# Gate and up projections of the feed-forward layers by one level of Strassen's scheme

## The chip, the cores and the metric

One Trainium2 chip, one of its cores. The metric is the device time of one launch in microseconds; the median of three runs of the kernel before is 3846.43 (3845.4 to 3850.24).

## What is computed

Three hybrid layers over 512 tokens of width 1024 in float32. Each has a large input projection, several sequence branches (state space, RWKV and HGRN in the first; mLSTM, grouped attention, windowed attention and differential attention in the other two), a gated merge with an output projection, and a feed-forward layer. The last of these is what matters here:

```python
h2 = rms_norm(x, norm2_g)
ffn = (jax.nn.silu(h2 @ w_ffn_gate) * (h2 @ w_ffn_up)) @ w_ffn_down
return x + ffn
```

with a hidden width of 2816, that is 22 tiles of 128. The first layer has the same form under other names.

## The kernel before

Activations lie with their channels on the 128 partitions and the 512 tokens along the free axis: `k.x` is 8 tiles of 128x512. A product in float32 accuracy is made of three passes (`three_passes`, L561): the upper part of the weights times the upper part of the activations, upper times lower, lower times upper (L563, L564, L565), where "upper" is the value rounded to the matmul's type (fp32r) and "lower" what is left. Weights come from HBM in chunks of 128x1024 (eight tiles of 128x128) into `k.raw`, four chunks deep (`Stream.load`, L468, issued by SyncE). ScalarE copies a chunk to its upper part (`make_hi`, L486), VectorE subtracts to get the lower part (`make_lo`, L492), each two chunks deep. A chunk is used once.

The gate/up stage is `scaled_products` (L4351): a step is one gate tile and one up tile of the hidden width, two steps to a body, 22 steps in a loop. TensorE makes 24 matmuls of 512 columns for the gate and 24 for the up tile. The norm's weight is multiplied into the activations ahead (`SplitAhead`, L1598, beside the output projection of the merge); the norm's factor per token, `rstd`, is applied afterwards: VectorE multiplies the gate out of PSUM by it (L4430), ScalarE applies Silu (L4409), GpSimd multiplies by `rstd` once more for the up side (L4452), VectorE multiplies by the up tile out of PSUM (L4442), ScalarE and VectorE split the hidden tile (L4413, L4435). `ScaledEnd` (L4303) does this for the last hidden tile inside the down projection.

The output projection `w_out` runs in `project` (L885), with `SquareSum` (L1457: squares on ScalarE, L1480; their sums on GpSimd, L1491) and `SplitAhead` (L1624 on ScalarE, L1633 on VectorE) beside it. Its last tile is left to the next stage: `LastTile` (L837) adds it there (L853), splits it and gives the sums of squares to TensorE (L877, L880). Each engine runs its instructions in the order in which the code lists them; semaphores are the only coupling between engines. Stages end in a change of block that all engines share.

## Time and profile before

| | |
|---|---|
| median of 3 runs | 3846.43 us |
| span of the profiled execution | 3844.5 us |
| TensorE busy | 3642.5 us, 95% |
| VectorE, ScalarE, GpSimd busy | 1980.4, 1634.2, 402.0 us |
| three gate/up stages | about 242 us each |

The launch's own time of the profiled execution is not printed beside its span; the median stands 1.9 us above that span. In the profile an engine's busy time is the sum of its recorded instructions. PE is TensorE, PEld its loads of weights, DVE VectorE, ACT ScalarE, POOL GpSimd, SP SyncE. A matmul's recorded duration includes its way through the array, so the distance between starts, not the duration, says what a matmul costs.

### The profile page before, as it was taken

What the parts mean: (1) busy time and instruction counts of PE and PEld (TensorE: products, weight loads), DVE (VectorE), ACT (ScalarE), POOL (GpSimd) and SP (SyncE); (2) the same over time, 40 slices, a digit from 0 to 9 for tenths busy, and PEclk for the clock granted to TensorE, in tenths of its full rate; (3) what the DMA queues carried; (4) which work ended last, traced back from release to release, by engine and by line L of the source; (5) the groups of instructions that cost most, each with busy time, mean ns of one, the idle gap of its engine ahead of it and who ended that gap; (6) DMA issues with size and microseconds to landing.
All of it is one profiled execution on the core that took longest, in us unless ns stands there. A gap on an engine that the chain in (4) does not pass through costs nothing. (4 is left out here: it accounts for less than half of the span.)

```text
span 3844.5 us, 52297 instructions
## 1 busy us (share of the span) xinstructions
PE 3642.5 (95%) x20532; PEld 2868.1 (75%) x20532; DVE 1980.4 (52%) x3166; ACT 1634.2 (43%) x2544; POOL 402.0 (10%) x353
## 2 busy tenths in 40 slices
PE   8898889969999999899999999999899999999998
PEld 6456777758878887677777788887687777788887
DVE  5879565584443334655545443333655545443332
ACT  5454432545333334456444433223456445433222
POOL 0027233000001111320000001100020000001100
PEclk9899889979999999999999999999999999999999
DMA  3012001203232232112212232333212212232232
GB/s 124 11 47 61 1 2 62 72 3 123 91 104 94 97 96 91 55 55 72 68 65 87 90 102 93 98 93 95 66 50 73 68 50 99 85 105 93 98 93 77
DMA packets 84161, 289.34 MB, mean 75 GB/s; under 512 B 9200, under 2 KB 9456, under 8 KB 82672
## 3 DMA queue, kind: packets, MB, share of 16 engines
q1 hardware_dynamic: 83520, 283.68, 23.1%
q8 instruction: 143, 2.34, 0.2%
q10 hardware_dynamic: 432, 2.78, 0.2%
q14 instruction: 66, 0.54, 0.0%
HBM read 284.32 MB, written 2.10 MB: 75 GB/s over the span
## 5 line engine op out<-in xcount | busy, mean ns | idle before, releaser
L492 DVE TENSOR_TENSOR weights_lo_r<-raw_weights,weights_hi_r 128x1024 fp32r<-128x1024 f32 (+2 forms) x554 | 637.9, 1152 | 1278.1 <-ACT weights_hi_r L486 1277.8
L486 ACT ACTIVATE weights_hi_r<-raw_weights 128x1024 fp32r<-128x1024 f32 (+2 forms) x554 | 546.7, 987 | 1263.6 <-PE ps L565 1212.5
L564 PE MATMUL ps<-xn_r,weights_hi_r 128*128 128x512 f32 x2688 | 1057.8, 394 | 0.0
L563 PE MATMUL ps<-xn_hi,weights_hi_r 128*128 128x512 f32 x1632 | 670.5, 411 | 46.1 <-DVE xn_r L558 18.3
L565 PE MATMUL ps<-xn_hi,weights_lo_r 128*128 128x512 f32 x1632 | 646.0, 396 | 0.0
L564 PEld LDWEIGHTS ps<-xn_r,weights_hi_r 128*128 128x128 f32 x2688 | 511.6, 190 | 106.1 <-issue 5.3
L563 PE MATMUL ps<-y_r,weights_hi_r 128*128 128x512 f32 x1200 | 469.6, 391 | 2.4 <-PEq L890 2.4
L565 PE MATMUL ps<-y_r,weights_lo_r 128*128 128x512 f32 x1200 | 466.9, 389 | 0.0
L563 PEld LDWEIGHTS ps<-xn_hi,weights_hi_r 128*128 128x128 f32 x1632 | 312.6, 192 | 141.7 <-issue 49.7
L565 PEld LDWEIGHTS ps<-xn_hi,weights_lo_r 128*128 128x128 f32 x1632 | 313.1, 192 | 69.0
L563 PEld LDWEIGHTS ps<-y_r,weights_hi_r 128*128 128x128 f32 x1200 | 225.2, 188 | 53.7 <-issue 6.4
L565 PEld LDWEIGHTS ps<-y_r,weights_lo_r 128*128 128x128 f32 x1200 | 225.3, 188 | 47.2
L563 PE MATMUL ps<-y_hi,weights_hi_r 128*128 128x512 f32 x576 | 227.9, 396 | 2.2 <-PEq L1134 1.9
L565 PE MATMUL ps<-y_hi,weights_lo_r 128*128 128x512 f32 x576 | 224.6, 390 | 0.0
L563 PE MATMUL ps<-hidden_hi,weights_hi_r 128*128 128x512 f32 x528 | 206.3, 391 | 1.0 <-PEq L4355 1.0
L564 PE MATMUL ps<-y_r,weights_hi_r 128*128 128x512 f32 x528 | 205.5, 389 | 0.0
L565 PE MATMUL ps<-hidden_hi,weights_lo_r 128*128 128x512 f32 x528 | 205.5, 389 | 0.0
L564 PE MATMUL ps<-hidden_r,weights_hi_r 128*128 128x512 f32 x528 | 205.5, 389 | 0.0
L1491 POOL TENSOR_TENSOR y<-y 128x512 f32<-128x512 f32 x18 | 23.3, 1294 | 1727.2 <-ACT y L1480 1727.2
L4452 POOL TENSOR_TENSOR y<-y 128x512 f32<-128x512 f32 x63 | 81.4, 1293 | 611.6 <-ACT y L4409 611.6
L563 PEld LDWEIGHTS ps<-y_hi,weights_hi_r 128*128 128x128 f32 x576 | 108.2, 188 | 28.3 <-DVE weights_lo_r L492 3.0
L565 PEld LDWEIGHTS ps<-y_hi,weights_lo_r 128*128 128x128 f32 x576 | 108.1, 188 | 23.1
(575 smaller groups left out, 5328.8 us busy)
## 6 DMA issues: line engine op xcount, KB each, us to landing
raw_weights<-in_w_ffn_dram SPq DMA_DIRECT2D x132, 512.0 KB, 3.7
raw_weights<-in_w_down_dram SPq DMA_DIRECT2D x48, 512.0 KB, 3.5
raw_weights<-in_w_out_dram SPq DMA_DIRECT2D x24, 512.0 KB, 3.5
raw_weights<-in_w_down_dram SPq DMA_DIRECT2D x24, 384.0 KB, 3.1
raw_weights<-in_w_hgrn_dram SPq DMA_DIRECT2D x16, 512.0 KB, 3.5
raw_weights<-in_w_mix_ssm_dram SPq DMA_DIRECT2D x16, 512.0 KB, 3.8
raw_weights<-in_w_a_qk_dram SPq DMA_DIRECT2D x16, 512.0 KB, 3.5
raw_weights<-in_w_mix_a_dram SPq DMA_DIRECT2D x16, 512.0 KB, 3.5
```

What stands on the lines that cost most here:

```text
L486: act.activation(self.k.w_hi[:, g % 2, 0:chunk.width], self.k.raw[:, slot, 0:chunk.width], ACT.Copy)\
L492: dve.tensor_tensor(self.k.w_lo[:, g % 2, 0:chunk.width], self.k.raw[:, slot, 0:chunk.width], self.k.w_hi[:, g % 2, 0:chunk.width].bitcast ...
L563: pe.matmul(out, w_hi, x_hi, start=start, stop=False)
L564: pe.matmul(out, w_hi, x_lo, start=False, stop=False)
L565: return pe.matmul(out, w_lo, x_hi, start=False, stop=stop)
L1491: pool.tensor_tensor(self.sums[:, n, :], self.sums[:, n, :], self.sq[:, kinds * (m % 2) + n, :], ALU.add)\
L4452: pool.tensor_tensor(gate[:, s, :], gate[:, s, :], rstd, ALU.mult).then_inc(gate_scaled, 1)
```

## The change

The gate and up projections of one step are taken as a 2 by 2 block product: weights in blocks (gate, up) by (lower, upper half of the 1024 channels), activations in blocks (lower, upper half of the channels) by (first, second 256 tokens). The seven products of the Strassen-Winograd form replace the eight. Each is 4 tiles of channels by three passes, 84 matmuls of 256 columns in a step.

- Of the activations, four combinations are needed: `t1` (a difference within the lower channel half) and `t3`, `t2`, `t4` (in `tri`). They are made beside `w_out` by `SplitSeven` in place of `SplitAhead`, and for the last tile by `SevenTile`; the weighted activation now is a tile of its own, from which upper and lower parts are split.
- Of the weights, four sums of 128x512 are made per step on GpSimd (`weight_sum`) and go through a ring of four slots. ScalarE and VectorE make upper and lower parts for five half-width blocks (`ring_part`; the fifth is the raw block of up and the upper channels) and for the whole gate row (`next_whole`).
- In PSUM, a product that enters several quarters is accumulated, copied out by ScalarE at three points of a step (`take_base`, `take_second`, `take_third`) into `held`, and VectorE forms the four quarters of gate and up from PSUM and `held`.
- The first multiplication by `rstd` reads and writes SBUF on VectorE (before: PSUM to SBUF); the product of gate and up has both inputs in SBUF. The second multiplication by `rstd` stays on GpSimd.
- The loops are written out. SyncE's loads wait for `sums_made`, `ring_ready` and `whole_ready` in place of `parts_ready`.
- `QuartersEnd` takes the place of `ScaledEnd`.

The core of the diff:

```diff
+class Seven:
+    PLACES = {"b11": ("low", 0), "t1": ("low", 1), "b21": ("mid", 0), "b22": ("mid", 1),
+              "t3": ("tri", 0), "t2": ("tri", 1), "t4": ("tri", 2)}
+    def __init__(self, low, mid, tri):
+        self.low, self.mid, self.tri = low, mid, tri
+        self.of = {"low": low, "mid": mid, "tri": tri}
+    def block(self, name, j):
+        kind, n = self.PLACES[name]
+        at = slice(n * HALF, (n + 1) * HALF)
+        return self.of[kind].hi[:, j, at], self.of[kind].lo[:, j, at]
+HALF = T // 2
+KH = KD // 2
...
+    def triple(self, dve, j, done, n):
+        t, b = self.seven.tri.full[:, j, :], self.seven.mid.full[:, j, :]
+        dve.scalar_tensor_tensor(out=t[:, 0:HALF], in0=self.x[:, j, HALF:T], scalar=self.k.col(self.weight, j),
+                                 in1=b[:, HALF:T], op0=ALU.mult, op1=ALU.subtract).then_inc(done, 1)
+        dve.wait_ge(done, n + 1)
+        dve.scalar_tensor_tensor(out=t[:, HALF:T], in0=self.x[:, j, 0:HALF], scalar=self.k.col(self.weight, j),
+                                 in1=t[:, 0:HALF], op0=ALU.mult, op1=ALU.subtract).then_inc(done, 1)
+        dve.wait_ge(done, n + 2)
+        dve.tensor_tensor(t[:, T:T + HALF], b[:, 0:HALF], t[:, HALF:T], ALU.subtract).then_inc(done, 1)
+    def scalar(self, act):
+        for m in range(KD):
+            if m < KD - 1:
+                act.wait_ge(self.tile_used, m + 1)
+                self.weigh(act, m, self.weighed)
+            if 1 <= m <= KH:
+                act.wait_ge(self.combined, m)
+                self.seven.low.make_hi(act, m - 1).then_inc(self.seven_hi, 1)
+            elif m > KH:
+                j = m - 1 - KH
+                act.wait_ge(self.weighed, m)
+                self.seven.mid.make_hi(act, j).then_inc(self.seven_hi, 1)
+                act.wait_ge(self.combined, KH + 3 * (j + 1))
+                self.seven.tri.make_hi(act, j).then_inc(self.seven_hi, 1)
+            yield
+    def vector(self, dve):
+        def low_parts(m):
+            if m < KH:
+                dve.wait_ge(self.seven_hi, m + 1)
+                self.seven.low.make_lo(dve, m).then_inc(self.seven_ready, 1)
+                return
+            j = m - KH
+            dve.wait_ge(self.combined, KH + 3 * (j + 1))
+            dve.wait_ge(self.seven_hi, KH + 2 * j + 1)
+            self.seven.mid.make_lo(dve, j).then_inc(self.seven_ready, 1)
+            dve.wait_ge(self.seven_hi, KH + 2 * j + 2)
+            self.seven.tri.make_lo(dve, j).then_inc(self.seven_ready, 1)
+        for m in range(KD):
+            if m:
+                dve.wait_ge(self.weighed, m)
+                if m <= KH:
+                    f = self.seven.low.full[:, m - 1, :]
+                    dve.tensor_tensor(f[:, HALF:T], f[:, 0:HALF], f[:, HALF:T], ALU.subtract).then_inc(self.combined, 1)
+                else:
+                    self.triple(dve, m - 1 - KH, self.combined, KH + 3 * (m - 1 - KH))
+            if m >= 2:
+                low_parts(m - 2)
+            yield
+        low_parts(KD - 2)
+        yield
...
-        sides = SquareSum(k.x, 1, squares), SplitAhead(k.x, norm, ahead, k.xn.lo)
+        sides = SquareSum(k.x, 1, squares), SplitSeven(k.x, norm, seven)
...
-def scaled_products(k, name, src, split, gate, rstd, opening):
+RING = 4
...
+def strassen_products(k, name, seven, split, gate, rstd, held, ring, opening):
...
+            for i in range(N):
+                for row in range(2):
+                    g = g0 + 2 * (i + 2) + row
+                    if g >= stream.stop():
+                        continue
+                    sp.wait_ge(sums_made, 4 * i + 3 + row)
+                    if row:
+                        sp.wait_ge(ring_ready, 5 * i + 5)
+                    elif i:
+                        sp.wait_ge(whole_ready, i)
+                    chunk = stream.plan[g]
+                    sp.dma_start(k.raw[:, g % AHEAD_RAW, 0:chunk.width],
+                                 k.dram[chunk.name][chunk.row, :, chunk.at:chunk.at + chunk.width])\
+                        .then_inc(stream.weights_in[g % AHEAD_RAW], 16)
...
+            def times(out, w_hi, w_lo, name, js=range(KH), start=False):
+                for j in js:
+                    x_hi, x_lo = seven.block(name, j)
+                    at = slice(j * P, (j + 1) * P)
+                    for n, (a, b) in enumerate(((w_hi, x_hi), (w_hi, x_lo), (w_lo, x_hi))):
+                        mm = pe.matmul(out, a[:, at], b, start=start and j == 0 and n == 0,
+                                       stop=j == KH - 1 and n == 2, skip_group_check=True)
+                return mm
...
+            pe.wait_ge(stream.parts_ready, g0 + 1)
+            times(out(0, 0), *whole(0), "b11", start=True).then_inc(whole_used, 1)
+            most, rest = range(KH - 1), range(KH - 1, KH)
+            times(out(0, 1), *whole(1), "b21", most, True)
+            pe.wait_ge(ring_ready, 1)
+            times(out(0, 3), *part(0), "t3", most, True)
+            pe.wait_ge(taken, 1)
+            pe.wait_ge(ring_ready, 2)
+            times(out(0, 0), *part(1), "t2", most)
+            pe.wait_ge(ring_ready, 3)
+            times(out(0, 2), *part(2), "b22", most, True)
+            opening.ready(pe)
+            times(out(0, 1), *whole(1), "b21", rest).then_inc(whole_used, 1)
+            times(out(0, 3), *part(0), "t3", rest).then_inc(ring_used, 1)
+            times(out(0, 0), *part(1), "t2", rest).then_inc(ring_used, 1)
+            times(out(0, 2), *part(2), "b22", rest).then_inc(ring_used, 1)
+            opening.sums(pe)
+            pe.wait_ge(taken, 2)
+            pe.wait_ge(ring_ready, 4)
+            times(out(0, 0), *part(3), "t1").then_inc(ring_used, 1)
+            for i in range(1, N):
+                n = 5 * i
+                pe.wait_ge(whole_ready, i)
+                if i >= 2:
+                    pe.wait_ge(taken, 3 * (i - 1))
+                times(out(i, 0), *whole(0), "b11", start=True).then_inc(whole_used, 1)
+                last_product(i - 1).then_inc(ring_used, 1)
+                pe.wait_ge(ring_ready, n + 1)
+                if i >= 2:
+                    pe.wait_ge(quarter_ready, 4 * (i - 1))
+                else:
+                    pe.wait_ge(logs, 1)
+                times(out(i, 3), *part(n), "t3", start=True).then_inc(ring_used, 1)
+                times(out(i, 1), *whole(1), "b21", start=True).then_inc(whole_used, 1)
+                pe.wait_ge(ring_ready, n + 2)
+                pe.wait_ge(taken, 3 * i + 1)
+                times(out(i, 0), *part(n + 1), "t2").then_inc(ring_used, 1)
+                pe.wait_ge(ring_ready, n + 3)
+                times(out(i, 2), *part(n + 2), "b22", start=True).then_inc(ring_used, 1)
+                pe.wait_ge(ring_ready, n + 4)
+                pe.wait_ge(taken, 3 * i + 2)
+                times(out(i, 0), *part(n + 3), "t1").then_inc(ring_used, 1)
+            last_product(N - 1).then_inc(stream.chunk_used, end - g0)
...
+            opening.weigh(act)
+            take_base(0)
+            ring_part(0)
+            ring_part(1)
+            ring_part(2)
+            opening.square(act)
+            ring_part(3)
+            take_second(0)
+            ring_part(4)
+            next_whole(1)
+            act.wait_ge(opening.sums_done, 1)
+            act.activation(rstd, bank(k.ps, 7), ACT.Ln, bias=k.const("eps")[:, 0:1], scale=1.0 / D).then_inc(logs, 1)
+            act.wait_ge(logs, 1)
+            act.activation(rstd, rstd, ACT.Exp, scale=-0.5).then_inc(rstd_ready, 1)
+            ring_part(5)
+            for i in range(1, N):
+                take_third(i - 1)
+                ring_part(5 * i + 1)
+                ring_part(5 * i + 2)
+                take_base(i)
+                act.wait_ge(scaled, i)
+                act.activation(gate[:, (i - 1) % 2, :], gate[:, (i - 1) % 2, :], ACT.Silu).then_inc(gate_ready, 1)
+                ring_part(5 * i + 3)
+                ring_part(5 * i + 4)
+                next_whole(i + 1)
+                take_second(i)
+                act.wait_ge(tile_ready, i)
+                split.make_hi(act, i - 1).then_inc(hi_ready, 1)
+                if i + 1 < N:
+                    ring_part(5 * i + 5)
+            take_third(N - 1)
...
+            def quarter(i, o, b, h, op):
+                dve.tensor_tensor(o, k.ps[:, 4 * (i % 2) + b, 0:HALF], h, op).then_inc(quarter_ready, 1)
+            def second_halves(i):
+                dve.wait_ge(taken, 3 * i + 3)
+                quarter(i, dst[:, i, HALF:T], 3, held_1, ALU.add)
+                quarter(i, gate[:, i % 2, HALF:T], 2, held_1, ALU.subtract)
+            def up_first(i):
+                dve.wait_ge(ring_used, 5 * i + 5)
+                quarter(i, dst[:, i, 0:HALF], 3, held_2, ALU.add)
+            opening.combine(dve)
+            ring_part(0)
+            for r in range(1, 5):
+                ring_part(r)
+            gate_first(0)
+            next_whole(1)
+            for i in range(1, N):
+                second_halves(i - 1)
+                ring_part(5 * i)
+                ring_part(5 * i + 1)
+                if i == 1:
+                    dve.wait_ge(rstd_ready, 1)
+                dve.wait_ge(quarter_ready, 4 * i - 1)
+                dve.tensor_tensor(gate[:, (i - 1) % 2, :], gate[:, (i - 1) % 2, :], rstd, ALU.mult).then_inc(scaled, 1)
+                ring_part(5 * i + 2)
+                up_first(i - 1)
+                ring_part(5 * i + 3)
+                ring_part(5 * i + 4)
+                dve.wait_ge(gate_scaled, i)
+                dve.wait_ge(quarter_ready, 4 * i)
+                dve.tensor_tensor(dst[:, i - 1, :], gate[:, (i - 1) % 2, :], dst[:, i - 1, :], ALU.mult)\
+                    .then_inc(tile_ready, 1)
+                gate_first(i)
+                next_whole(i + 1)
+                dve.wait_ge(hi_ready, i)
+                split.make_lo(dve, i - 1).then_inc(lo_ready, 1)
+            second_halves(N - 1)
...
+            def weight_sum(n, a, b):
+                if n >= RING:
+                    pool.wait_ge(ring_used, n - 3)
+                pool.tensor_tensor(slot(n)[0], a, b, ALU.add).then_inc(sums_made, 1)
+            def first_two(i):
+                arrived(pool, i, 0)
+                arrived(pool, i, 1)
+                weight_sum(5 * i, raw(i, 0, 0), raw(i, 1, 0))
+                pool.wait_ge(sums_made, 4 * i + 1)
+                weight_sum(5 * i + 1, slot(5 * i)[0], raw(i, 1, 1))
+            def third(i):
+                pool.wait_ge(sums_made, 4 * i + 2)
+                weight_sum(5 * i + 2, slot(5 * i + 1)[0], raw(i, 0, 1))
+            def fourth(i):
+                weight_sum(5 * i + 3, raw(i, 1, 0), raw(i, 1, 1))
+            first_two(0)
+            third(0)
+            fourth(0)
+            first_two(1)
+            for i in range(1, N):
+                g = gate[:, (i - 1) % 2, :]
+                third(i)
+                fourth(i)
+                pool.wait_ge(gate_ready, i)
+                pool.tensor_tensor(g, g, rstd, ALU.mult).then_inc(gate_scaled, 1)
+                if i + 1 < N:
+                    first_two(i + 1)
```

## Rows read from the trace of the kernel before

**Rows 1.** The page: busy time, granted clock in 40 slices, DMA issues.

```profile
PE 3642.5 (95%) x20532; PEld 2868.1 (75%) x20532; DVE 1980.4 (52%) x3166; ACT 1634.2 (43%) x2544; POOL 402.0 (10%) x353
...
PEclk9899889979999999999999999999999999999999
...
raw_weights<-in_w_ffn_dram SPq DMA_DIRECT2D x132, 512.0 KB, 3.7
```

**Rows 2.** Busy time by stretch, gate/up stage 1: length, PE, PEld, DVE, ACT, POOL, clock.

```profile
1134.60:1376.30 241.70, 241.41 (x1060) 198.88 (x1060) 93.14 (x109) 77.23 (x93) 27.14 (x21) 1.00 0.29 95
```

**Rows 3.** Timeline (start us, us, instruction), two matmuls ten apart in that stage.

```profile
1200.21 0.39 PE L565 MATMUL ps<-y_r,weights_lo_r 128*128 128x512 f32 x1
...
1202.48 0.39 PE L563 MATMUL ps<-y_r,weights_hi_r 128*128 128x512 f32 x1
```

**Rows 4.** Groups by line in that stage: count, busy us, mean ns, idle before.

```profile
L492 DVE TENSOR_TENSOR weights_lo_r<-raw_weights,weights_hi_r 128x1024 fp32r<-128x1024 f32 x44 | 53.9, 1226 | 143.4 <-ACT weights_hi_r L486 143.4
L486 ACT ACTIVATE weights_hi_r<-raw_weights 128x1024 fp32r<-128x1024 f32 x44 | 46.7, 1061 | 124.4 <-PE ps L565 122.8 <-PEq L890 1.7
L4452 POOL TENSOR_TENSOR y<-y 128x512 f32<-128x512 f32 x21 | 27.1, 1293 | 203.9 <-ACT y L4409 203.9
...
L4409 ACT ACTIVATE y<-y 128x512 f32<-128x512 f32 x21 | 13.3, 632 | 37.9 <-DVE y L4430 37.8
```

**Rows 5.** Timeline of TensorE in the mLSTM branch, matmuls of 256 columns.

```profile
1629.84 0.28 PE L564 MATMUL ps<-qk_r,qk_hi 128*128 128x256 f32 x1
...
1630.07 1.05 PE L3607 MATMUL ps<-v_tok,qk_raw 128*128 128x129 f32 x8
...
1635.07 0.28 PE L564 MATMUL ps<-qk_r,qk_hi 128*128 128x256 f32 x1
...
1635.31 1.05 PE L3607 MATMUL ps<-v_tok,qk_raw 128*128 128x129 f32 x8
```

**Rows 6.** Timeline of VectorE in the first gate/up stage.

```profile
1203.09 1.23 DVE L492 TENSOR_TENSOR weights_lo_r<-raw_weights,weights_hi_r 128x1024 fp32r<-128x1024 f32 x1 [3.62 <-ACT weights_hi_r L486]
1204.23 0.68 DVE L4435 TENSOR_TENSOR hidden_r<-hidden,hidden_hi  x1
1204.84 0.68 DVE L4442 TENSOR_TENSOR hidden<-y,ps 128x512 f32 x1
```

**Rows 7.** Groups by line over the whole span, 256 columns out of PSUM.

```profile
L2875 DVE TENSOR_TENSOR transfer<-ps,factors 128x256 f32<-128x256 f32 x32 | 12.1, 419 | 15.4 <-PE ps L2661 15.4
...
L2755 ACT ACTIVATE transfer<-ps 128x256 f32<-128x256 f32 x32 | 10.5, 381 | 40.0 <-PE ps L2670 40.0
```

**Rows 8.** Timeline of GpSimd and VectorE in w_out and, from 1398, w_down.

```profile
1105.27 1.29 POOL L1491 TENSOR_TENSOR y<-y 128x512 f32<-128x512 f32 x1 [485.18 <-ACT y L1480]
1105.84 1.27 DVE L1633 SCALAR_TENSOR_TENSOR xn_r<-x_again,cols,y_r 128x512 fp32r<-128x512 f32 x1 [1.31 <-ACT y_r L1624]
...
1398.00 0.96 DVE L492 TENSOR_TENSOR weights_lo_r<-raw_weights,weights_hi_r 128x768 fp32r<-128x768 f32 x1 [0.72 <-ACT weights_hi_r L486]
...
1410.30 3.09 POOL L1491 TENSOR_TENSOR xn<-xn 128x512 f32<-128x512 f32 x2 [45.53 <-ACT xn L1480]
...
1411.48 0.75 DVE L1633 SCALAR_TENSOR_TENSOR y_r<-x_again,norm_product,y_r 128x512 fp32r<-128x512 f32 x1 [1.93 <-ACT y_r L1624]
...
1412.96 1.25 DVE L492 TENSOR_TENSOR weights_lo_r<-raw_weights,weights_hi_r 128x768 fp32r<-128x768 f32 x1 [0.72 <-ACT weights_hi_r L486]
```

**Rows 9.** Timeline in the RWKV branch: VectorE with a PSUM input beside GpSimd.

```profile
560.47 1.90 POOL L2949 TENSOR_TENSOR factors<-consts,chunk_ends 128x1024 f32<-128x1024 f32 x1
560.98 1.29 DVE L2855 TENSOR_TENSOR raw_weights<-ps,consts 128x512 f32<-128x512 f32 x2 [2.46 <-PE ps L2601]
```

**Rows 10.** Timeline at the start of the first gate/up stage.

```profile
1136.90 0.74 DVE L867 SCALAR_TENSOR_TENSOR xn_r<-x_again,cols,y_r 128x512 fp32r<-128x512 f32 x1
...
1141.53 1.28 ACT L4403 ACT_TABLE_LOAD   x1
```

**Rows 11.** Busy time by stretch in the mLSTM branch, as in group 2.

```profile
1621.00:1627.00 6.00, 5.77 (x24) 4.36 (x24) 3.48 (x7) 1.66 (x4) 1.75 (x4) 0.67 0.01 3
```

More of the change, by code:

```diff
@@ L4271, in diff_attention, with merge @@
                      bias_of=lambda h, i: slope[:, h, 384 - P * i:896 - P * i], neg_lambda=lam[:, 5:6])
-def merge(k, branches, w_out, norm, ahead, squares, func=ACT.Sigmoid, begun=None):
+def merge(k, branches, w_out, norm, seven, squares, func=ACT.Sigmoid, begun=None):
     with ExitStack() as ctx:
@@ L4332, in vector @@
             return
+        o = self.parts.full[:, self.tile, :]
+        dve.tensor_tensor(self.gate, self.gate, self.rstd, ALU.mult).then_inc(self.scaled, 1)
         dve.wait_ge(self.k.stream.chunk_used, self.used)
-        dve.tensor_tensor(self.gate, bank(self.k.ps, 2), self.rstd, ALU.mult).then_inc(self.scaled, 1)
+        dve.tensor_tensor(o[:, 0:HALF], self.k.ps[:, self.bank, 0:HALF], self.held, ALU.add)\
+            .then_inc(self.quarter_ready, 1)
         dve.wait_ge(self.gate_ready, 1)
@@ new lines, in whole, with part, out, last_product @@
+            def whole(half):
+                at = slice(half * W, (half + 1) * W)
+                return k.w_hi[:, first, at], k.w_lo[:, first, at]
+            def part(n):
+                _, lo, hi = slot(n)
+                return hi, lo
+            def out(i, b):
+                return k.ps[:, 4 * (i % 2) + b, 0:HALF]
+            def last_product(i):
+                pe.wait_ge(ring_ready, 5 * i + 5)
+                pe.wait_ge(quarter_ready, 4 * i + 2)
+                return times(out(i, 3), *part(5 * i + 4), "t4")
@@ L4458, in feed_forward @@
-def feed_forward(k, spare, early, w_ffn, w_down, opening, weight=None, final=None, product=None):
+        return QuartersEnd(split, gate[:, (N - 1) % 2, :], rstd, held_2, 4 * ((N - 1) % 2) + 3, end)
+def feed_forward(k, spare, early, seven, w_ffn, w_down, opening, weight=None, final=None, product=None):
     with ExitStack() as ctx:
```

235 lines of the change are left out of this document (146 added, 89 removed).

## The prediction

> **What bounds the kernel now.** I read the share of busy time first: TensorE is busy 95% of the span, VectorE 52%, ScalarE 43%, GpSimd 10%, and in the 40 slices the granted clock of the feed-forward stages is at full speed [rows 1]. Then I went to the stage that is changed. There are three gate/up stages; the first runs from 1134.6 to 1376.3 us, 241.7 us, in which TensorE is busy 241.4, VectorE 93, ScalarE 77, GpSimd 27 us [rows 2]. All of it is a run of 22 x 2 x 24 = 1056 matmuls of 512 columns. Their starts stand 0.227 us apart (ten of them from 1200.21 to 1202.48) [rows 3], so a pair of tiles gate/up (a "step" below) costs 48 x 0.227 = 10.88 us, 22 steps 239.4 us, and the sums of squares and the change of block the rest. The stage is bound by TensorE alone: before VectorE's L492 stand 143 us of idle time in this stage, before GpSimd's only operation, L4452, 204 us [rows 4].
>
> **TensorE after.** A step becomes seven products of 4 blocks x 3 passes: 84 matmuls of 256 columns instead of 48 of 512. In columns that is 7/8. What a 256-column matmul costs I take from the only such three-pass matmuls at full clock: two in a row take from 1629.84 to the next instruction at 1630.07, and two more from 1635.07 to 1635.31: four spacings, mean 0.1175 us [rows 5]. 84 x 0.1175 = 9.87 us. So TensorE alone would give 1.01 us per step, 66 steps, 67 us. The Trainium skill (TensorE: Matmul & The Clock Gate, LDWEIGHTS (loading the stationary operand)) puts a load of 128 columns at 107 ns, which lies under the 0.117 us shown; by that page the loads, now 84 in place of 48 per step, would stay hidden, an estimate of 9.0 us of loading against 9.87.
>
> **VectorE after, per step.** With inputs both in SBUF: five lower parts of half-width weights (128x512), one of a whole row (128x1024), the factor on the gate, gate times up, the lower part of the hidden tile. That is eight of 512 and one of 1024 columns. With a PSUM input: four quarters of 256 columns. In the row of starts the 1024 form takes 1.14 us to the next start and the 512 form 0.61 [rows 6]; a 256 form with PSUM input lasts 0.42 [rows 7], 0.35 to the next start with the same overlap. Sum 8 x 0.61 + 1.14 + 4 x 0.35 = 7.42 us, under 9.87. ScalarE: five copies of 512 at 0.63, one of 1024 at 1.06, three of 256 out of PSUM at 0.38, Silu and the hidden tile's copy at 0.63 each: 6.6 us [rows 4, 7]. GpSimd: four weight sums and the second factor, five additions or multiplications of 128x512 at 1.29 [rows 4], 6.5 us. Each engine by itself would keep pace.
>
> **But VectorE and GpSimd don't run by themselves.** In w_out, GpSimd's sum of squares starts at 1105.27 and ends at 1106.56; VectorE's L1633, two SBUF inputs, is recorded from 1105.84 to 1107.11, 1.27 us for a form that takes 0.75 at 1411.48, where GpSimd is just ending. It ends 0.55 after GpSimd's end: one data pass. The other way round, at 1411.48 VectorE is first: of GpSimd's two additions, 3.09 us together instead of 2.59, the second ends 1.16 us after VectorE's end, and the lower part of the weights behind it (1412.96) takes 1.25 us instead of the 0.96 at 1398.00, ending 0.82 after GpSimd's [rows 8]. An operation of VectorE with a PSUM input beside GpSimd keeps its time (two in 1.29 us beside a 1.90 us GpSimd operation) [rows 9]. So whichever starts first holds something whole, and the other waits. The gate/up stage of the kernel before hardly shows it, because GpSimd has one operation in 10.88 us and VectorE is then idle. The Trainium skill (SBUF — State Buffer, Who interferes with whom) says just this: a VectorE instruction with two SBUF inputs and a GpSimd instruction that reads SBUF take turns at one port, for the whole instruction. The trace agrees (0.55, 1.16 and 0.82 us).
>
> **The step with this in it.** Each GpSimd operation that falls into a busy stretch of VectorE turns a spacing of 0.61 into 0.55 + 1.16 = 1.71 us, so adds 1.10. All five: 7.42 + 5.5 = 12.9 us, the upper end. The lower end lets nothing but the held passes count: 8 x 0.55 + 1.09 (0.82 for 768 columns, 0.27 more for 256) + 5 x 1.16 = 11.3 us, with every PSUM operation beside GpSimd. Both lie above the 9.87 of TensorE and above the 10.88 of before. Which in between: the first weight sum that needs a free slot is released by the end of the product "t1", the same event that releases ScalarE's third copy and then the two PSUM quarters of second_halves, so these 0.7 us do lie beside it; the others meet SBUF operations as a rule. 12.9 - 0.7 = 12.2 us. As a second way to it I laid steps out, with the waits of the code. The first of them, from the end of "t1": third copy to 0.5, the two quarters to 1.4, the first sum beside them to 1.4; two ring parts and the factor to 3.35; the second sum (released by the last product, 2.8) takes the port from 3.3 to 4.5, the third ring part ends at 5.05; the second factor on GpSimd holds it to 6.1, the fourth ring part ends at 6.7, the fifth at 7.3; the sum released by "t2" (7.0) holds to 8.45, the product gate times up ends at 9.0; the sum released by "b22" (8.4) holds to 10.15, and the whole row's lower part ends at 11.25. "t1" of this step has ended at 9.8, so "b11" of the next waits 1.5 us, and then the last product for the quarters until 13.4, 12.0 after its start one step earlier. The next three steps by the same rules gave 12.8, 10.6 and 13.0, mean of the four 12.1. I take 12.2.
>
> **Start of the stage.** Before: TensorE goes straight on, since 21 matmuls cover the last tile's chain add, upper part, lower part (done at 1137.64, some 3 us into the stage), and the three table loads of 1.28 us on ScalarE for Ln, Exp and Silu have cover [rows 10]. After: GpSimd makes four sums in a row (first result 1.3 us in), while VectorE needs the last tile's addition, three combinations and the first ring part (5 SBUF operations, each meeting a sum). The first combination is ready at 1.5, waits for the second sum (2.6) and ends at 2.95; with a sum of 1.16 between each pair the second ends at 4.4, the third at 5.85, and the ring part for "t3" at 6.4, where TensorE wants it at 2.4. The parts of the last tile follow at 7.9 and the ring parts at 8.5, 9.1 and 9.7; TensorE then has 4.2 us of products kept back for the last tile and the two sums of squares (1.7) to do, and "t1" ends at 15.0; Ln and Exp with their table loads stand on ScalarE ahead of the third copy, so the last product of step 0 runs from 18.8 to 20.2. Then 21 x 12.2 = 256.2, and 0.7 for the change of block: 277.1 us against 241.7, +35.4 us a stage, three stages +106.
>
> **w_out before it.** VectorE per tile there: an addition, the lower part of the weights and one more operation, of 5.44 us between them. For the tiles 5 to 7 it becomes 0.61 + 1.14 + three combinations of 256 (0.4 each with their own waits) + lower parts of 512 and 768 (0.61, 0.88) + one GpSimd sum in the way (1.1) = 5.5 us and a little for waits: up to 0.3 a tile late, three tiles, with the waits behind it 1.3 us a stage, +4. Loads from HBM keep their number and size. SyncE issues each row two steps ahead, behind waits for the weight sums and lower parts instead of parts_ready; with some 3.7 us to land [rows 1] against over 12 to its use they are covered, and without that cover a step would gain those 3.7 us.
>
> **Sum.** 3 x (35.4 + 1.3) = +110 us. The profiled execution spans 3844.5 us; the median of the runs is 3846.4, 1.9 above it. Its own span becomes 3955, the median 3957 us.
>
> **The rivals.**
> (a) TensorE stays the bound and the change gives what its column count says. For it: no engine's own sum passes 9.87, and the cases of rows 8 stand outside this stage. Against: all three forms in question are seen to wait. It would give a start of 17.9 us (ends of the same layout without the port), 21 x 9.87 and 0.7: 225.9, -16 a stage, with the 4 us in w_out about 3803 us. Chance 0.11.
> (b) The waits couple: a ring of four slots makes GpSimd wait for TensorE, which waits for VectorE, which waits for ScalarE in its order; then VectorE idles besides being blocked. A step of 13.5 us, from where VectorE's stream has over 0.6 us of idle time per step, gives 3 x 21 x 1.3 = 82 more: about 4039 us. In my layout such idle time is in one step of four. Chance 0.10. The granted clock belongs here: after an idle stretch of some 5 us it was 0.67 in the mean of the next 6 us [rows 11]. My gaps are 1 to 4 us; one fall at the start of each stage costs some 3 us.
> (c) The change doesn't do what it says, since a 256-column matmul is paced by its weight load: at 0.13 us a step is 10.9 us even without the port, about 3860 us with the slower starts. Rows 5 speak against it. Chance 0.03.
> (d) The forecast: the port between VectorE and GpSimd is the bound. Chance 0.76.
>
> **How the numbers follow.** The ends of the step, 11.3 and 12.9, give 3957 - 63 x 0.9 = 3900 and 3957 + 63 x 0.7 = 4001; the start of the stage may be 7 us less or more in each, 21 together. That makes 3879 to 4022, wherein lies nearly all of (d); (b) is partly inside. 3870 to 4025 leaves out (a), (c) and half of (b), about 2 in 10. A measurement of this kernel can tell about 0.2%, 8 us, from no change. Faster is (a) alone, 0.11; the same is a part of (c), 0.02; slower is the rest, 0.87.
>
> **What would show it.** In the profile after: VectorE's lower parts of 128x512 with a mean well over 0.68 us (nearer 1.0) and GpSimd's additions over 1.29; busy time of VectorE in the stage above 200 us of some 275; TensorE idle 2 us and more per step, released by VectorE; 256-column matmuls 0.117 us apart wherever they run in a row. The forecast is wrong if VectorE's operations keep 0.68 beside GpSimd's, or if the steps are 9.9 us apart; its size is wrong if the start of the stage doesn't show "t3" waiting some 4 us.

## The result, and the profile after

The changed kernel takes 3943.33 us (median of 4 runs, 3943.14 to 3943.64), the kernel before on the same chip 3845.91 (4 runs, 3841.56 to 3850.24): ratio 1.0251, 95% interval 1.0237 to 1.0266. It is slower by 97.4 us; 110 were forecast. The profiled execution spans 3941.5 us against 3844.5, which is 97.0 more.

The page after, the lines that answer to [rows 1] (busy time, slices of VectorE and GpSimd, granted clock), and the costliest of the new groups:

```profile
span 3941.5 us, 58231 instructions
...
PE 3627.5 (92%) x22908; PEld 2950.9 (75%) x22908; DVE 2495.3 (63%) x3754; ACT 1850.8 (47%) x3042; POOL 872.3 (22%) x617
...
DVE  5879565573469954755545469963655545459972
...
POOL 0026332000037720310000027720020000017730
PEclk9899989979999999999999999999899999999999
...
L4711 DVE TENSOR_TENSOR weights_lo_r<-weights_lo,weights_hi_r 128x512 fp32r<-128x512 f32 x132 | 156.4, 1194 | 0.0
```

TensorE's share fell from 95 to 92%, and VectorE shows three places at 9 in the slices, each beside GpSimd at 7: the gate/up stages. The lower part of 128x512 has a mean of 1.19 us; the same form takes 0.68 in [rows 6]. The granted clock by slices differs from before in two digits only (a 9 for an 8, an 8 for a 9); what it does at the start of a stage is too short for a slice and is read further down.

Busy time by stretch (length, PE, PEld, DVE, ACT, POOL, clock, DMA share, GB/s): two steps of stage 1, then the three gate/up stages, which answer to [rows 2].

```profile
1227.01:1250.55 23.54, 21.12 (x168) 20.37 (x168) 23.54 (x27) 12.50 (x22) 17.14 (x11) 1.00 0.29 90
...
1136.76:1405.85 269.09, 238.41 (x1852) 228.86 (x1853) 258.00 (x289) 143.55 (x249) 184.19 (x109) 0.98 0.28 86
...
2337.60:2605.46 267.86, 237.52 (x1852) 227.93 (x1853) 257.99 (x288) 143.56 (x249) 184.17 (x109) 0.99 0.27 87
...
3535.50:3803.46 267.96, 237.62 (x1852) 227.95 (x1853) 258.01 (x288) 143.54 (x249) 183.65 (x109) 0.99 0.27 87
```

VectorE is busy in all 23.54 us of the two steps: it is the engine that sets the pace. The whole-row lower part (L4719) starts every 11.78 us in the mean, by turns 11.02 and 12.54. Where TensorE waits, the groups by line of that stage say whom for:

```profile
L4564 PE MATMUL ps<-xn_hi,weights_hi_r 128*128 128x256 f32 x260 | 76.5, 294 | 23.2 <-DVE weights_lo_r L4719 16.2 <-PEq L890 6.6
...
L4711 DVE TENSOR_TENSOR weights_lo_r<-weights_lo,weights_hi_r 128x512 fp32r<-128x512 f32 x44 | 52.1, 1194 | 0.0
...
L4780 POOL TENSOR_TENSOR weights_lo<-raw_weights 128x512 f32<-128x512 f32 x23 | 35.0, 1523 | 47.7 <-PE ps L4564 40.4 <-issue 7.4
...
L4727 DVE TENSOR_TENSOR y<-ps,y 128x256 f32<-128x256 f32 x44 | 18.0, 409 | 0.2 <-PE ps L880 0.2
```

The quarters out of PSUM keep their time (409 ns against 419 in [rows 7]); everything of VectorE with two SBUF inputs is stretched, and GpSimd's sums too. The timeline (start, duration) of one step of VectorE, then of GpSimd, shows where:

```profile
1228.90 0.41 DVE L4727 TENSOR_TENSOR y<-ps,y 128x256 f32<-128x256 f32 x1
...
1230.43 0.68 DVE L4760 TENSOR_TENSOR y<-y 128x512 f32<-128x512 f32 x1
1231.04 1.79 DVE L4711 TENSOR_TENSOR weights_lo_r<-weights_lo,weights_hi_r 128x512 fp32r<-128x512 f32 x1
1232.75 0.41 DVE L4727 TENSOR_TENSOR hidden<-ps,y 128x256 f32<-128x256 f32 x1
1233.08 1.45 DVE L4711 TENSOR_TENSOR weight_ring_r<-weight_ring,weight_ring_hi 128x512 fp32r<-128x512 f32 x1
1234.45 0.68 DVE L4711 TENSOR_TENSOR weight_ring_r<-raw_weights,weight_ring_hi 128x512 fp32r<-128x512 f32 x1
...
1235.99 1.98 DVE L4719 TENSOR_TENSOR weights_lo_r<-raw_weights,weights_hi_r 128x1024 fp32r<-128x1024 f32 x1
1237.89 1.77 DVE L558 TENSOR_TENSOR hidden_r<-hidden,hidden_hi 128x512 fp32r<-128x512 f32 x1
...
1240.26 1.70 DVE L4711 TENSOR_TENSOR weights_lo_r<-weights_lo,weights_hi_r 128x512 fp32r<-128x512 f32 x2
```

```profile
1230.88 1.39 POOL L4780 TENSOR_TENSOR weight_ring<-raw_weights 128x512 f32<-128x512 f32 x1 [2.79 <-PE ps L4564]
1232.23 1.75 POOL L4806 TENSOR_TENSOR y<-y 128x512 f32<-128x512 f32 x1
1235.29 1.60 POOL L4780 TENSOR_TENSOR weights_lo<-raw_weights 128x512 f32<-128x512 f32 x1 [1.31 <-PE ps L4564]
1236.97 2.15 POOL L4780 TENSOR_TENSOR weights_lo<-weights_lo,raw_weights 128x512 f32<-128x512 f32 x1
```

These lines let the price of a meeting be read. Undisturbed, a form of 512 takes 0.60 to the next start and the one of 1024 takes 1.14. At 1231.04 the spacing is 1.71, 1.11 over. At 1233.08 it is 1.37, 0.77 over: the quarter that ran just ahead (0.33) lay beside GpSimd's pass. At 1235.99 it is 1.90, 0.76 over, again behind one quarter; at 1237.89 it is 1.70. At 1240.26, behind two quarters, two forms take 1.62 instead of 1.20, 0.42 over. So each GpSimd operation costs VectorE 1.10 us, less 0.33 for each quarter that runs beside it. In two steps (23.56 us) ten operations meet VectorE and six of the eight quarters lie beside one: 10 x 1.10 - 6 x 0.33 = 9.0 us, and what is left, 14.56, is 7.28 us a step for VectorE by itself. The undisturbed spacings give the same without this subtraction: 8 x 0.60 + 1.14 + 4 x 0.33 = 7.26.

By stage (us), by starts of matmuls: w_out from its second one to the first of gate/up, gate/up to the first of w_down, w_down to its own last one:

| | before | after |
|---|---|---|
| w_out, layers 1 to 3 | 44.40, 44.35, 44.34 | 50.52, 50.50, 50.50 |
| gate/up | 241.73, 241.71, 241.71 | 269.09, 267.86, 267.96 |
| w_down | 119.56, 119.54, 122.91 | 119.57, 119.57, 122.92 |
| w_down's last matmul to the next w_out's second | 760.8, 758.25 | 761.68, 759.97 |
| the first w_out's second matmul | 1090.23 | 1086.24 |

That is 18.4 in w_out and 79.8 in gate/up; the parts that the change doesn't touch give -4.0 and +2.6 (the part ahead of the first w_out is the same in all kernels of this case, and their profiled executions reach it anywhere between 1083 and 1093, so the -4.0 is no gain of the change). 96.8 of 97.0 us are placed.

In w_out the loss is at its end, and so is the wait at the start of gate/up. TensorE's last matmul of w_out, VectorE's queue behind it, the first matmul of gate/up and the one that waits for `t3`'s weights:

```profile
1129.74 0.39 PE L565 MATMUL ps<-y_hi,weights_lo_r 128*128 128x512 f32 x1
...
1129.25 1.40 DVE L1693 TENSOR_TENSOR y<-xn,y 128x256 f32<-128x256 f32 x1
...
1132.04 0.47 DVE L1687 SCALAR_TENSOR_TENSOR y<-x_again,cols,xn 128x256 f32<-128x256 f32 x1
...
1135.48 0.95 DVE L558 TENSOR_TENSOR y_r<-y,y_r 128x768 fp32r<-128x768 f32 x1
...
1136.76 0.55 PE L4564 MATMUL ps<-xn_hi,weights_hi_r 128*128 128x256 f32 x1 [6.63 <-PEq L890]
...
1143.86 0.80 PE L4564 MATMUL ps<-y_r,weights_hi_r 128*128 128x256 f32 x2 [3.02 <-DVE weights_lo_r L4711]
```

TensorE is done at 1130.13. VectorE then still has the end of a combination, the lower parts of tile 4, the three combinations of tile 6 and the lower parts of tiles 5 and 6, until 1136.43; all engines share the change of block, so TensorE stands for 6.63 us. Before, it stood for 0.48 us at this place:

```profile
1134.63 0.47 PE L563 MATMUL ps<-y_r,weights_hi_r 128*128 128x512 f32 x1 [0.48 <-PEq L890]
```

The difference, 6.15 us, is all that w_out lost.

### The profile page after: what moved, and what is told of

Its sections match the earlier page's. It is cut to its first block and busy times, and to the rows that moved or that the text cites. A ratio compares the mean times of both kernels' runs of the same rounds, so it can differ in the third digit from the quotient of the medians.

```text
span 3941.5 us, 58231 instructions
## 1 busy us (share of the span) xinstructions
PE 3627.5 (92%) x22908; PEld 2950.9 (75%) x22908; DVE 2495.3 (63%) x3754; ACT 1850.8 (47%) x3042; POOL 872.3 (22%) x617
## 5 line engine op out<-in xcount | busy, mean ns | idle before, releaser
L492 DVE TENSOR_TENSOR weights_lo_r<-raw_weights,weights_hi_r 128x1024 fp32r<-128x1024 f32 (+2 forms) x422 | 476.1, 1129 | 876.6 <-ACT weights_hi_r L486 876.5
L564 PE MATMUL ps<-xn_r,weights_hi_r 128*128 128x512 f32 x1632 | 645.8, 396 | 0.0
L563 PEld LDWEIGHTS ps<-xn_hi,weights_hi_r 128*128 128x128 f32 x1632 | 312.4, 191 | 141.4 <-issue 49.9
L564 PEld LDWEIGHTS ps<-xn_r,weights_hi_r 128*128 128x128 f32 x1632 | 313.6, 192 | 64.6 <-issue 4.6
L4564 PE MATMUL ps<-xn_hi,weights_hi_r 128*128 128x256 f32 x780 | 229.9, 295 | 69.6 <-DVE weights_lo_r L4719 48.7
L4564 PE MATMUL ps<-xn_r,weights_hi_r 128*128 128x256 f32 x780 | 222.7, 286 | 0.0
L4564 PE MATMUL ps<-xn_hi,weights_lo_r 128*128 128x256 f32 x780 | 222.1, 285 | 0.0
L4564 PEld LDWEIGHTS ps<-xn_hi,weights_hi_r 128*128 128x128 f32 x780 | 151.4, 194 | 83.6 <-DVE weights_lo_r L4719 62.5
L564 PE MATMUL ps<-y_r,weights_hi_r 128*128 128x512 f32 x528 | 206.6, 391 | 0.0
L4564 PE MATMUL ps<-y_r,weights_hi_r 128*128 128x256 f32 x840 | 162.3, 292 | 27.9 <-DVE hidden L4727 19.5
L4711 DVE TENSOR_TENSOR weights_lo_r<-weights_lo,weights_hi_r 128x512 fp32r<-128x512 f32 x132 | 156.4, 1194 | 0.0
```

Of the source, the lines that this page charges most:

```text
L492: dve.tensor_tensor(self.k.w_lo[:, g % 2, 0:chunk.width], self.k.raw[:, slot, 0:chunk.width], self.k.w_hi[:, g % 2, 0:chunk.width].bitcast ...
L563: pe.matmul(out, w_hi, x_hi, start=start, stop=False)
L564: pe.matmul(out, w_hi, x_lo, start=False, stop=False)
L4564: mm = pe.matmul(out, a[:, at], b, start=start and j == 0 and n == 0, stop=j == KH - 1 and n == 2, skip_group_check=True)
L4711: dve.tensor_tensor(lo, raw(i, 1, 1) if r == 4 else full, hi.bitcast(F32), ALU.subtract)\
```

## The experiments

The theory is that VectorE bounds the step because GpSimd's operations hold an SBUF port that it needs. The rivals were that the products themselves pace the step, that the waits between the engines do, or that VectorE is simply too full. The runs come from two chips, on which the kernel before takes 3850.86 and 3844.56 us; no run of the changed kernel stands beside them, so launch times are compared with the kernel before, and the changed kernel is compared by stages and steps of the profile.

**GpSimd's weight sums without reading SBUF.** The sums are left out; a fill of the same slot stands in their place, with all waits.

```diff
-                pool.tensor_tensor(slot(n)[0], a, b, ALU.add).then_inc(sums_made, 1)
+                pool.memset(slot(n)[0], 0.0).then_inc(sums_made, 1)
```

> GpSimd fills the four slots of the ring with zeros in place of the weight sums: same places, same waits, same count of GpSimd instructions, but they read no SBUF (the sums are left out, so the output isn't the reference's). Port theory (VectorE operations with two SBUF inputs and GpSimd operations that read SBUF take turns): only the second factor is left to collide, 7.42 + 1.1 = 8.5 us of VectorE per step, under TensorE's 9.87, so steps of 9.9 to 10.1 us instead of 11.76 and lower parts of 128x512 at a mean near 0.68 us instead of 1.19; launch about 3943 - 63 x 1.8 = 3830 us or less. Rival, VectorE's own stream is the bound whatever GpSimd does (it is recorded busy 23.5 of 23.5 us in two steps): steps stay over 11.5 us. Rival, the pace of 84 weight loads: steps stay at 11.8 us.

3836.81 us (one run; before 3850.86 on that chip), the stages 231.0 us, the step 10.08. Groups by line from 1160 to 1360:

```profile
L4711 DVE TENSOR_TENSOR weights_lo_r<-weights_lo,weights_hi_r 128x512 fp32r<-128x512 f32 x40 | 33.9, 857 | 2.8 <-ACT weights_hi_r L4639 2.8
...
L4780 POOL MEMSET weights_lo<- 128x512 f32 x40 | 21.0, 526 | 64.1 <-PE ps L4564 64.1
```

With every wait and every instruction of VectorE in place, 1.7 us a step are gone, and VectorE has idle time again. So the waits and VectorE's own work don't make 11.78. The lower parts have a mean of 0.86 and not the 0.68 that was expected; the timeline shows why. One lower part runs beside a fill and keeps 0.69, the next meets the second factor, which GpSimd still multiplies in this kernel, and takes 1.37:

```profile
1211.96 0.69 DVE L4711 TENSOR_TENSOR weights_lo_r<-weights_lo,weights_hi_r 128x512 fp32r<-128x512 f32 x1
...
1213.26 1.37 DVE L4711 TENSOR_TENSOR weights_lo_r<-weights_lo,weights_hi_r 128x512 fp32r<-128x512 f32 x1 [0.28 <-ACT weights_hi_r L4639]
```

```profile
1211.97 0.53 POOL L4780 MEMSET weights_lo<- 128x512 f32 x1 [2.00 <-PE ps L4564]
1212.79 1.30 POOL L4806 TENSOR_TENSOR y<-y 128x512 f32<-128x512 f32 x1 [0.29 <-ACT y L4692]
```

But a fill is also shorter (0.53 us) than a sum; the next kernel takes that away.

**The sums with one input.** The sums are again left out: each slot is filled with one of its inputs times 1.0.

```diff
-                pool.tensor_tensor(slot(n)[0], a, b, ALU.add).then_inc(sums_made, 1)
+                pool.tensor_scalar(slot(n)[0], a, 1.0, None, ALU.mult).then_inc(sums_made, 1)
```

> GpSimd's four sums become multiplications of the first input by one (one SBUF input, sums left out, so the output isn't the reference's). Such a form took 1.57 us alone in the trace of before, longer than the addition's 1.29, but VectorE operations beside it lost only 0.3 to 0.45 us instead of 1.09. Port theory: 7.42 + 4 x 0.4 + 1.1 = 10.1 us of VectorE, steps of 10.1 to 10.5 us, although GpSimd is busier. Rival, the loop of waits through the ring and GpSimd's own length set the step: GpSimd's 6.5 us per step grow by 1.1, steps of 12 us or more.

3844.74 us (one run, same chip), the stages 236.0 to 237.0, the step 10.3. Groups by line in the same stretch:

```profile
L4780 POOL TENSOR_SCALAR weights_lo<-raw_weights 128x512 f32<-128x512 f32 x19 | 32.5, 1710 | 14.3 <-PE ps L4564 14.3
```

GpSimd's operation lasts 1.71 us, longer than the sum with two inputs (1.52), and the step is still 1.5 us shorter. So it isn't GpSimd's length or lateness either; what counts is what it reads while VectorE wants to read. The timeline of VectorE and GpSimd shows the smaller price:

```profile
1211.07 1.12 DVE L558 TENSOR_TENSOR hidden_r<-hidden,hidden_hi 128x512 fp32r<-128x512 f32 x1
...
1211.03 1.49 POOL L4780 TENSOR_SCALAR weights_lo<-weight_ring 128x512 f32<-128x512 f32 x1
```

1.12 instead of 0.68: 0.44 us over, the most that a meeting costs in the two steps around it (0.08 to 0.44), where an operation with two inputs costs 1.10.

**All five of GpSimd's operations on VectorE.** The whole computation; the diff is cut to one of the five, and the calls are placed between VectorE's own.

```diff
+            def fourth(i):
+                dve.wait_ge(sums_made, 4 * i + 3)
+                weight_sum(5 * i + 3, raw(i, 1, 0), raw(i, 1, 1))
...
+                dve.wait_ge(gate_ready, i)
+                dve.tensor_tensor(g, g, rstd, ALU.mult).then_inc(gate_scaled, 1)
...
-                pool.tensor_tensor(g, g, rstd, ALU.mult).then_inc(gate_scaled, 1)
```

> All five GpSimd operations of a step (four sums, second factor) are moved to VectorE, GpSimd does nothing in the stage; the computation is whole. VectorE gets 5 x 0.61 us more work. Port theory: 7.42 + 3.05 = 10.5 us per step with no turns to take, steps of 10.5 to 10.7 instead of 11.76, the start of the stage some 4 us shorter: 3943 - 63 x 1.2 - 12 = about 3855 us. Rival, VectorE is simply overloaded and GpSimd relieves it: steps of 12 us or more, over 3955 us.

3877.99 us (one run, same chip), the stages 244.2 to 245.0, the step 10.68: a step is 1.10 us shorter than in the changed kernel, with five instructions more on the engine that bounds it. 3855 were expected. The steps came out in the range that was given, at its upper end, but the start of a stage is 0.6 to 1.0 us shorter, not 4, and in this profile the first w_out begins 5.9 us later than in that of the changed kernel. A sum costs VectorE 0.60 us if it makes it itself and 1.10 if GpSimd makes it beside it. In the stretch from 1160 to 1360 the lower part is back at its own time:

```profile
L4711 DVE TENSOR_TENSOR weights_lo_r<-weights_lo,weights_hi_r 128x512 fp32r<-128x512 f32 x38 | 26.2, 690 | 3.0 <-ACT weights_hi_r L4639 1.3
```

It is still slower than before (+0.7%): w_out keeps its 50.5 us, and VectorE, busy 20.93 us of two steps of 21.35, is still the bound. (The order of VectorE's instructions had to change with this kernel too, so it alone would not tell a better order from a free port; the kernels above and below it do.)

**The second factor deferred.** `rstd` is one number per token, and the down projection is linear. So, on the kernel with all on VectorE, the second multiplication goes from the 22 hidden tiles to the 8 output tiles of w_down, where VectorE has room. The whole computation is kept.

```diff
-                dve.tensor_tensor(g, g, rstd, ALU.mult).then_inc(gate_scaled, 1)
-                ring_part(5 * i + 3)
-                dve.wait_ge(gate_scaled, i)
...
+                        if factor:
+                            dve.tensor_tensor(factor[1], bank(k.ps, (job.t0 + s) % 4), factor[0], ALU.mult)\
+                                .then_inc(factored, 1)
+                            dve.wait_ge(factored, i * job.body + s + 1)
+                            dve.tensor_tensor(o, o, factor[1], ALU.add).then_inc(tile_used, 1)
```

> As the kernel with all on VectorE, and the second factor per token is taken out of the hidden tiles and put once on each of the eight output tiles of the down projection (the product is linear in it): one operation of 128x512 less per step, one with a PSUM input more per down tile, where VectorE is idle most of 15 us. The computation is whole. Port theory: VectorE 7.42 + 4 x 0.61 = 9.86 us per step, TensorE 9.87: steps of 9.9 to 10.3 us; 3943 - 63 x 1.65 - 12 = about 3827 us, faster than the kernel before (3846) by some 19 us although w_out keeps its 6 us a stage. If the VectorE stream is the bound by its count of instructions and waits rather than by the sum of its spacings, steps stay over 10.9 us and the launch over 3870.

3839.0 us (5 runs, 3834.25 to 3839.76) against 3850.86 (8 runs): ratio 0.9964, interval 0.9950 to 0.9978. 3827 were expected, with 9.87 us for TensorE's step; at the 10.08 measured here that sum gives 13 us more, 3840. The stages take 232.1 to 232.5 us, w_down the same as before within 0.05. Busy time by stretch, two steps and the whole first stage:

```profile
1225.00:1245.16 20.16, 20.16 (x171) 20.16 (x170) 19.74 (x36) 12.38 (x22) 0.00 (x0) 1.00 0.33 106
...
1138.87:1370.99 232.12, 226.53 (x1852) 224.24 (x1853) 219.07 (x376) 142.13 (x249) 0.00 (x0) 0.99 0.32 100
```

Now TensorE is busy throughout: this is the step that the seven products are worth by themselves, 10.08 us. It is also the price of a matmul, 10.08 / 84 = 0.120 us, where I had 0.1175 from [rows 5]. The timeline shows the same in a run of them (nine matmuls apart):

```profile
1230.00 0.40 PE L4581 MATMUL ps<-y_r,weights_hi_r 128*128 128x256 f32 x2
...
1231.08 0.28 PE L4581 MATMUL ps<-xn_hi,weights_hi_r 128*128 128x256 f32 x1
```

**Another order beside w_out.** On the kernel above: an output tile is added as soon as it is there, its combinations follow at once, and its lower parts one tile later, so that less is left over at the end. The diff is cut to the order of VectorE.

```diff
+                        if late:
...
+                                dve.tensor_tensor(o, o, bank(k.ps, (job.t0 + p) % 4), ALU.add).then_inc(tile_used, 1)
+                            stream.run_ahead(stream.make_lo, dve, job, i, last, p, AHEAD_PARTS)
+                            next(side_pieces, None)
+                            continue
...
-            if m >= 2:
-                low_parts(m - 2)
...
+                low_parts(m - 1)
```

> The deferred kernel with another order of the work beside w_out alone: VectorE adds a tile before it makes the next chunk's lower part, combines a tile in that tile's own turn instead of one turn later, and makes the lower parts one turn later instead of two. No operation is added or taken away. Backlog theory (TensorE stands 6.6 us before the gate/up stage, because the change of block waits until VectorE has worked off two tiles of combinations and lower parts): VectorE then ends some 2.5 us after TensorE instead of 6.3, w_out 46.7 to 47.5 us instead of 50.5, three stages 9 to 11 us, and less of the stage's start at the lower clock: about 3827 us against 3839. Rival, the 6 us are the change of block itself or the GpSimd sum that VectorE waits for: w_out stays within 1 us of 50.5.

3825.17 us (4 runs, 3820.89 to 3829.76) against 3844.56 (7 runs): ratio 0.9949, interval 0.9933 to 0.9966. By its ratio it is the fastest of all, 0.5% under the kernel before and 3% under the changed one; the interval overlaps that of the kernel above (0.9950 to 0.9978), so what the order is worth is read from the stage. w_out takes 46.70 us in each layer. The timeline at its end, VectorE's last lower part and TensorE's first product:

```profile
1130.46 0.95 DVE L558 TENSOR_TENSOR y_r<-y,y_r 128x768 fp32r<-128x768 f32 x1
...
1131.74 0.55 PE L4593 MATMUL ps<-xn_hi,weights_hi_r 128*128 128x256 f32 x1 [2.83 <-PEq L899]
```

6.63 us of idle time have become 2.83; the 3.80 between them are the whole gain of w_out, 50.50 - 46.70. So what costs time in w_out is the amount left in VectorE's queue at the end, not its rate per tile.

**The sums of squares beside w_out.** In the changed kernel, the additions of `SquareSum` are left out and replaced by a fill of 1.0.

```diff
-                pool.tensor_tensor(self.sums[:, n, :], self.sums[:, n, :], self.sq[:, kinds * (m % 2) + n, :], ALU.add)\
-                    .then_inc(self.added, 1)
+                pool.memset(self.sums[:, n, :], 1.0).then_inc(self.added, 1)
```

> The changed kernel, with GpSimd's sums of squares beside w_out and w_down replaced by a fill of the same tile (they read no SBUF; the sums are left out, so the output isn't the reference's). Rival of the backlog theory, turns at the port in w_out are the 6 us: w_out falls from 50.5 us by the 0.95 us of each collided combination, 2 us or more. Backlog theory: only the collision nearest the end can count, as VectorE has idle time before the others: w_out 49.5 to 50.5 us, the gate/up stages unchanged at 268.

3941.16 us (one run), w_out 48.95 in place of 50.5; gate/up takes 268.5 to 269.8, 0.6 to 0.7 us more than in the changed kernel. The 1.55 us gained lie between the two accounts that were set against each other: 49.5 to 50.5 us was expected for w_out if the backlog alone counts, 48.5 or less if the meetings do. So of the 6.1 us that w_out lost, GpSimd's additions have a part of 1.55, and the order of the work one of 3.8 (the kernel before this one). The two were not tried together, so whether the parts add up isn't shown. The last combination of a tile (L1693), 1.40 us beside an addition of GpSimd, is 0.42 here.

**The first factor moved to GpSimd.** In the changed kernel, one more operation goes from VectorE to GpSimd, which is idle for 27% of a step.

```diff
-                dve.wait_ge(quarter_ready, 4 * i - 1)
-                dve.tensor_tensor(gate[:, (i - 1) % 2, :], gate[:, (i - 1) % 2, :], rstd, ALU.mult).then_inc(scaled, 1)
...
+                pool.wait_ge(quarter_ready, 4 * i - 1)
+                pool.tensor_tensor(g, g, rstd, ALU.mult).then_inc(scaled, 1)
```

> The changed kernel with the first multiplication by the norm's factor on GpSimd instead of VectorE; the computation is whole. Port theory: in the steps of 11.76 us the five GpSimd operations cost VectorE 11.76 - 7.42 = 4.34 us, 0.87 each; VectorE has 0.61 less of its own and one more operation to meet: 6.81 + 6 x 0.87 = 12.0 us a step, the launch 3943 + 63 x 0.27 = 3960 us. Rival, VectorE's own count of work is the bound: steps of 11.2 us, 3908 us.

3989.43 us (one run; before 3844.56 on that chip), the step 12.60, the stages 284.3 to 285.6. Taking 0.60 us of work off the engine that bounds the step makes the step 0.82 longer. The way was expected, the size was not: 12.0 us and 3960 were on record, from a mean price of 0.87 per operation. The price read above, which was put together afterwards, gives it: 7.28 - 0.60 for VectorE itself, six operations at 1.10, less the two quarters that lie beside them in this trace, 12.6 us. Groups by line, 1160 to 1360:

```profile
L4711 DVE TENSOR_TENSOR weights_lo_r<-weights_lo,weights_hi_r 128x512 fp32r<-128x512 f32 x32 | 44.9, 1421 | 0.0
...
L4801 POOL TENSOR_TENSOR y<-y 128x512 f32<-128x512 f32 x16 | 26.8, 1673 | 20.7 <-DVE y L4727 20.7
```

## Why the prediction was right, and where it wasn't

**TensorE's own saving, 9.87 us a step.** It measured 10.08 in the step that TensorE bounds. The spacing of 0.1175 came from two pairs of matmuls [rows 5]; in long runs of them it is 0.120. Against the 0.227 of a 512-column matmul [rows 3] this is 5.7% more per column, so 7/8 of the columns gave 0.80 us a step in place of the 1.01 that I took. Since TensorE didn't set the step, this did not enter the forecast, but rival (a) was priced too low by it: 63 steps x 0.21 = 13 us, and the 4 us that it allowed for w_out were 18. 3803 would have been some 3830; the kernel with the fills, which is this case, took 3836.8.

**VectorE by itself, 7.42 us.** It measured 7.28 (7.26 by the sum of the undisturbed spacings).

**The port between VectorE and GpSimd.** This was the step on which the sign hung, and it held. The 1.10 us per operation from [rows 8] is 1.11 at 1231.04, and the three kernels in which GpSimd fills, reads one input or does nothing bring the step to 10.08, 10.3 and 10.68. That the PSUM operations lie beside it, from [rows 9], held too, only more often: I subtracted two quarters a step, 0.7 us; three of four lie there, 1.0. With the 7.26 of the spacings that is 7.26 + 5.5 - 1.0 = 11.8, and 11.78 was measured; I had 12.2. (The 7.28 was itself got from 11.78, so a sum with it would prove nothing.) My four steps laid out by hand (12.0, 12.8, 10.6, 13.0) had the alternation, but not its size (12.54 and 11.02). 63 steps x 0.42 = 26 us of overestimate.

The Trainium skill (SBUF — State Buffer, Who interferes with whom) has the two engines take turns for the whole instruction. For two-input operations the runs agree, 1.10 us per meeting. For a one-input operation of GpSimd, which by the Trainium skill would hold the port as long, VectorE was late by 0.44 us beside a 1.49 us instruction; the measurement decides.

**Start of the stage.** I had the last product of step 0 end at 20.2 us. Taking 21 steps and 0.7 us off the stages leaves 21.0 in the first and 19.8 and 19.9 in the other two, so the size held. `t3`'s wait was 3.0 us, not 4. But its parts were others: the clock is not in my sum (only rival (b) has a price for it, one fall of some 3 us a stage), and it fell twice. After 6.6 us without work the granted clock was 0.53 in the first 3.2 us of the stage, nearly all of it at the lower of the two levels (1.2 GHz), with the matmuls 0.213 us apart; after `t3`'s wait it was 0.50 again, for 6.14 us in the first stage and 3.40 in the second:

```profile
1136.76:1140.00 3.24, 3.24 (x16) 3.24 (x17) 2.41 (x3) 1.02 (x3) 2.19 (x2) 0.53 0.00 0
...
1143.86:1150.00 6.14, 6.14 (x27) 6.00 (x28) 3.22 (x5) 1.22 (x3) 0.00 (x0) 0.50 0.13 50
...
2344.70:2348.10 3.40, 3.40 (x15) 3.26 (x16) 3.22 (x5) 1.23 (x3) 0.00 (x0) 0.50 0.20 78
```

13 matmuls at 0.093 more each are 1.2 us a stage; the 27 of the second fall are 2.5 us in the first stage, and 12 fewer of them, 1.1 us, are nearly all of the difference between the first stage (269.09) and the second (267.86). The 20.2 us had nothing for this, so that they came out so near is in part luck: by this reckoning other terms in them were too long by about as much.

**w_out, +1.3 us a stage.** This was wrong: +6.1, and 18.4 in place of 4 in all. The failed step is "per tile there: ... up to 0.3 a tile late". I compared VectorE's work with the time of a tile, and by that it does keep pace: TensorE runs on to 1130.13. But its work lags by more than a tile, and at the end of the stage what is left must be finished before any engine goes on. Before, VectorE was done 0.15 us after TensorE there, and TensorE stood for 0.48 us. The other order gave back 3.8 us of this, and without GpSimd's additions 1.55 were gone.

The two errors are of opposite sign, 26 us too much in the steps and 14 too little in w_out, so the total is nearer (97.4 against 110) than its parts deserve; that is luck.

**Rivals.** (b), coupled waits, is out for the steps: VectorE is busy in every part of two steps. Of the first stage's 269.09 us it is idle for 11.1, at both ends of the stage alone; the longest wait there, 5.15 us for a copy of ScalarE, is of (b)'s kind, but comes once a stage. (c), a pace set by the weight loads at 0.13 us, is out at 0.120; that the spacing per column is above that of 512 columns is so, but why was not tried.

**Rows that I had named beforehand.** Lower parts near 1.0 us: 1.19. GpSimd's additions over 1.29: 1.52 and 1.75. VectorE over 200 us: 258. TensorE idle 2 us and more per step: it lost 11.78 - 10.08 = 1.7, less than I had named.

What stays open: why 256-column matmuls are 0.120 us apart in long runs, whether the 20 us at the start of the stage can be shortened, and whether w_out's two parts, GpSimd's additions and the order, add up; none was tried.

## What to carry to other kernels

Before moving elementwise work to an idle GpSimd, ask whether VectorE is busy with two-input SBUF operations meanwhile: here each such operation cost VectorE 1.10 us, more than the 0.60 of doing it there itself. A factor per token that stands ahead of a linear projection can be applied behind it, on fewer tiles (8 in place of 22). And where a stage ends for all engines at once, count what is still in the slowest queue then, not only whether that queue keeps pace.

## What the runs showed of the hardware that I had not expected

- A GpSimd operation with one SBUF input of 128x512 costs VectorE 0.08 to 0.44 us where the one with two inputs costs 1.10, though it lasts as long (a mean of 1.71 us against 1.52). A fill of GpSimd's, which reads nothing, costs nothing: 0.69 us for the lower part beside it.
- The loss is the same whichever operation of VectorE is hit (1.09 to 1.11), and each 0.33 us quarter out of PSUM beside the GpSimd pass takes just its own time off it: 0.77 behind one, 0.42 behind two.
- The granted clock fell to its lower level not only after 6.63 us without a matmul but also after 3.02 and 2.73 us, early in the stage, and stayed there for 6.14 and 3.40 us while TensorE was busy throughout.
- 256-column matmuls: 0.120 us apart in long runs, 0.1175 in pairs; 0.213 at the lower clock.
